# Attention by key heads, with divisions on GpSimd, in one step of a two-layer decoder

## What is computed

```python
def sink_softmax(s, mask, sink):
    s = jnp.where(mask, s, -jnp.inf)
    m = jnp.maximum(jnp.max(s, axis=-1, keepdims=True), sink)
    p = jnp.exp(s - m)
    return p / (jnp.sum(p, axis=-1, keepdims=True) + jnp.exp(sink - m))
# prompt: 4 blocks of 128 queries, each against its own block of keys and the block before
o = einsum(softmax(q k * scale), v);  x = x + o @ w_o
```

## Time and profile before

| | us |
|---|---|
| median of 3 runs | 3200.64 |
| lowest, highest | 3191.85, 3200.99 |
| the profiled execution: its own time | 3202.49 |
| its span, first to last instruction | 3200.7 |
| end of last query tile to first W_O matmul | 1654 to 1801 |

### The profile page before, as it was taken

The page is one execution under the profiler, slowest core; times in us unless marked ns, Lnnn a source line. Parts: engine busy times, 40 slices in busy tenths (PEclk is TensorE's granted clock), DMA queues, the critical chain, the costliest instruction groups (busy, mean ns, idle before and its releaser), DMA issues.

```text
span 3200.7 us, 46734 instructions
## 1 busy us (share of the span) xinstructions
PE 3069.8 (96%) x17222; PEld 2780.8 (87%) x17222; DVE 2551.4 (80%) x4953; ACT 1382.4 (43%) x2559; POOL 1746.1 (55%) x1160
## 2 busy tenths in 40 slices
PE   7879999999999999999888889999999999999997
PEld 7879999999998888888685789999999988888886
DVE  7755999977775999999567358989877759999987
ACT  2522343477764333333344223343777653333332
POOL 4543488887775444443130223788877755544442
PEclk9989999999999999999887899999999999999998
DMA  3212499999999999999130022799999999999993
GB/s 106 77 53 91 128 340 337 339 397 393 393 392 373 401 400 399 401 397 351 53 95 1 27 67 80 274 348 342 371 400 387 395 370 394 399 401 400 398 400 138
DMA packets 286579, 920.92 MB, mean 288 GB/s; under 512 B 27344, under 2 KB 77392, under 8 KB 282688
## 3 DMA queue, kind: packets, MB, share of 16 engines
q1 hardware_dynamic: 154336, 415.63, 35.9%
q0 software_dynamic: 111280, 404.77, 33.4%
q10 hardware_dynamic: 20736, 97.53, 7.4%
HBM read 817.34 MB, written 102.38 MB: 287 GB/s over the span
## 4 chain that ended last, share of the span: by engine, by line
PE 77%; DVE 16%; DMA 3%; POOL 2%; issue 1%; ACT 1%; DVEq 0%; ACTq 0%; SPq 0%
PE ps L1689 34%; PE ps L1637 22%; PE ps L1563 11%; PE ps L1669 5%; POOL low L604 2%; DMA raw<-uT 1%; PE ps L1811 1%; DVE xn L948 1%; DVE xl L941 1%; DVE cand L1218 1%; DVE cand L1225 1%; DVE slot L1231 1%; PE ps L1765 1%; PE ps L1800 1%; DVE rowsB L1129 1%
## 5 line engine op out<-in xcount | busy, mean ns | idle before, releaser
L762 ACT ACTIVATE high<-raw 128x1024 fp32r<-128x1024 f32 x512 | 542.7, 1060 | 992.2 <-PE ps L1689 665.9
L1637 PE MATMUL ps<-xh,high 128*128 128x384 f32 x2048 | 699.1, 341 | 14.8 <-POOL low L604 14.6
L604 POOL TENSOR_TENSOR low<-raw,high 128x1024 fp32r<-128x1024 f32 x256 | 614.2, 2399 | 167.2 <-ACT high L762 160.5
L1637 PE MATMUL ps<-xh,low 128*128 128x384 f32 x2048 | 687.4, 336 | 0.0
L1637 PE MATMUL ps<-xl,high 128*128 128x384 f32 x2048 | 686.2, 335 | 0.0
L1689 PE MATMUL ps<-high,hh 128*128 128x512 f32 x1536 | 483.5, 395 | 7.9 <-DVE low L1301 7.9
L1689 PE MATMUL ps<-low,hh 128*128 128x512 f32 x1536 | 481.1, 394 | 0.0
L1689 PE MATMUL ps<-high,hl 128*128 128x512 f32 x1536 | 480.3, 393 | 0.0
L595 POOL DMA_INDIRECT rowsA<-v,pick x192 | 271.3, 1413 | 296.9 <-DVE ps L1136 288.8
L1637 PEld LDWEIGHTS ps<-xh,high 128*128 128x128 f32 x2048 | 386.1, 189 | 20.8 <-POOL low L604 19.8
L595 POOL DMA_INDIRECT rowsB<-v,pick x192 | 240.2, 1251 | 271.0 <-DVE ps L1136 255.6
(11 more groups left out here) (279 smaller groups left out, 5043.5 us busy)
## 6 DMA issues: line engine op xcount, KB each, us to landing
raw<-uT SPq DMA_DIRECT2D x256, 512.0 KB
raw<-v SPq DMA_DIRECT2D x256, 512.0 KB
gate_dram<-gblk ACTq DMA_DIRECT2D x24, 2048.0 KB
gt<-gate_dram SPq DMA_DIRECT2D x32, 1536.0 KB
s_dram<-sring ACTq DMA_DIRECT2D x120, 384.0 KB
sring<-s_dram SPq DMA_DIRECT2D x120, 384.0 KB
raw<-wts SPq DMA_DIRECT2D x74, 512.0 KB, 3.6
rowsB<-u,pick POOLq DMA_INDIRECT x192
```

Source lines behind the costliest of these rows:

```text
L604: pool.tensor_tensor(low[:, m % 4], raw[:, m % 4], high[:, (m + 2) % 3].bitcast(F32), ALU.subtract).then_inc(sem("lo_ready"), 1)
L762: act.activation(high[:, (m + 2) % 3], tile_raw(m), ACT.Copy).then_inc(sem("hi_ready"), 1)
L1637: ins = pe.matmul(ps[:, m % 2, 0:DN], w[:, c], x[:, c, 0:DN], start=(c == 0 and k == 0), stop=(c == NC - 1 and k == 2))
```

## The change

Units run by key heads: `kv, n = divmod(u, NQB)`, so the units of block 0 are 0, 4, 8 and 12. Their absent half is neither filled, reduced, exponentiated, transposed nor copied. `sbank` swaps its pairs. Scores wait for the rotation of their own key head's two tiles alone. GpSimd multiplies by the reciprocals, and takes the samples' maximum off. `MIX_AT` is 7, two samples a step. `sample_keep` runs in steps 9 and 11. Chunks 0 to 5 are released in step 12 and split in steps 13, 14 and 15 (`SPLIT`), two chunks each. The negated sinks are made once.

```diff
-EXP_AT, SUM_AT_UNIT, TURN_AT, MIX_AT, KEEP_AT = 3, 4, 5, 8, 12
+EXP_AT, SUM_AT_UNIT, TURN_AT, MIX_AT, KEEP_AT, SPLIT = 3, 4, 5, 7, (9, 11), (13, 14, 15)
...
-            return ps[:, 4 * (u % 2):4 * (u % 2) + 2, :]
+            return ps[:, 4 * ((u + 1) % 2):4 * ((u + 1) % 2) + 2, :]
...
+            def weigh(k):
+                p, m = pr[:, k % PRS], sm[:, k % PRS]
+                lo = 0 if k % NQB else WIN
+                pool.wait_ge(sem("p_sum"), k + 1)
+                pool.tensor_tensor(p[:, :, lo:], p[:, :, lo:],
+                                   m[:, 5, 0:GRP].unsqueeze(2).broadcast_to([P, GRP, 2 * WIN - lo]), ALU.mult
+                                   ).then_inc(sem("p_ready"), 1)
+            def weigh_samples(k):
+                if k == EXP_AT:
+                    pool.wait_ge(sem("smax_ready"), 1)
+                    pool.tensor_tensor(pss[:, :, :], pss[:, :, :],
+                                       smS[:, 0].unsqueeze(2).broadcast_to([P, NB, WIN + TS]), ALU.subtract
+                                       ).then_inc(sem("smax"), 1)
+                elif k == SUM_AT_UNIT:
+                    pool.wait_ge(sem("s_sum"), 1)
+                    pool.tensor_tensor(pss[:, :, :], pss[:, :, :],
+                                       smS[:, 5].unsqueeze(2).broadcast_to([P, NB, WIN + TS]), ALU.mult
+                                       ).then_inc(sem("s_ready"), 1)
...
+                if l == 1:
+                    split_weights(W_K, W_O + 2)
+                    for k in range(UNITS):
+                        weigh(k)
+                        weigh_samples(k)
+                    lo = W_O + 2
                 split_weights(lo, hi)
...
+                    if u in SPLIT:
+                        c = 2 * SPLIT.index(u)
+                        split_x(X_O, c, c + 2)
+                split_x(X_O, 2 * len(SPLIT), NC)
...
-                    if not n:
-                        chain.did(dve.memset(p[:, :, 0:WIN], BIG))
-                    chain.did(dve.tensor_reduce(m[:, 0, 0:GRP], p, X, ALU.max))
+                    chain.did(dve.tensor_reduce(m[:, 0, 0:GRP], p[:, :, lo:], X, ALU.max))
...
                 for u in range(UNITS):
-                    normalise(u)
+                    inverse(u)
                     for k in items_due(u):
                         item(k)
...
+                    if u in KEEP_AT:
+                        sample_keep(KEEP_AT.index(u))
+                    if u in SPLIT:
+                        c = 2 * SPLIT.index(u)
+                        for i in range(c, c + 2):
+                            low_half(X_O, i)
+                    if u == SPLIT[0] - 1:
+                        whole(2 * len(SPLIT), u)
                 keep(UNITS - 1)
-                sample_keep(1)
+                whole(NC - 2 * len(SPLIT), UNITS)
+                for c in range(2 * len(SPLIT), NC):
                     low_half(X_O, c)
...
-                pe.wait_ge(sem("roped"), 2 + NC)
...
+                    if n == 0:
+                        pe.wait_ge(sem("roped"), 2 + 2 * (kv + 1))
...
-                    if u >= MIX_AT:
-                        sample_mix(u - MIX_AT)
+                    if MIX_AT <= u < MIX_AT + NB // 2:
+                        sample_mix(2 * (u - MIX_AT))
+                        sample_mix(2 * (u - MIX_AT) + 1)
```

More of the change, by code:

```diff
@@ L321, in decoder @@
         smS = st.take("smS", [P, 6, NB])
+        nsink = st.take("nsink", [P, NH + 1])
         st = Span(nc, free_at, SB_HI)
@@ L656, in high_weight, with split_x @@
                 act.activation(high[:, w % 2], raw[:, w % 2], ACT.Copy).then_inc(sem("qh_ready"), 1)
-            def split_x(k):
-                for c in range(NC):
+            def split_x(k, lo=0, hi=NC):
+                for c in range(lo, hi):
                     act.wait_ge(sem("x_whole"), k * NC + c + 1)
@@ L1394, in attention @@
                 ob = xn
+                chain.did(dve.tensor_scalar(nsink[:, 0:NH], prm[:, P_SINK:P_SINK + NH], -1.0, None, ALU.mult))
+                chain.settle()
                 dve.wait_ge(sem("tile_done"), D_O)
                 def scale_max(k, u):
-                    n, kv = divmod(u, NKV)
+                    kv, n = divmod(u, NQB)
                     p, m = pr[:, u % PRS], sm[:, u % PRS]
@@ L1427, in normalise @@
                     chain.settle()
[L1428 to L1431, removed]
+                    dve.reciprocal(m[:, 5, 0:GRP], m[:, 4, 0:GRP]).then_inc(sem("p_sum"), 1)
                 def keep(u):
-                    n, kv = divmod(u, NKV)
+                    kv, n = divmod(u, NQB)
                     dve.wait_ge(sem("p_out"), u + 1)
@@ L1459, in sample_max, with sample_inverse @@
                     chain.settle()
[L1460 to L1466, removed]
+                    dve.tensor_scalar(smS[:, 3], smS[:, 0], -1.0, prm[:, P_SKS:P_SKS + 1], ALU.mult, ALU.add
+                                      ).then_inc(sem("smax_ready"), 1)
+                def sample_inverse():
                     dve.wait_ge(sem("sexp"), 2)
@@ L1471, in sample_normalise @@
                     chain.settle()
[L1472 to L1476, removed]
+                    dve.reciprocal(smS[:, 5], smS[:, 4]).then_inc(sem("s_sum"), 1)
                 def sample_keep(bb):
@@ L1488, in sample_keep, with whole @@
                     ins.then_inc(sem("s_kept"), 1)
+                def whole(n, u):
+                    dve.wait_ge(sem("s_kept"), 2)
+                    dve.wait_ge(sem("o_copied"), u)
+                    chain.settle()
+                    dve.memset(mark[:, :], 0.0).then_inc(sem("x_whole"), n)
                 def item(k):
@@ L1506, in attention @@
                     if u == SUM_AT_UNIT:
-                        sample_normalise()
-                    if u == KEEP_AT:
-                        sample_keep(0)
-                keep(UNITS - 1)
-                sample_keep(1)
[L1512 to L1516, removed]
+                        sample_inverse()
+                    if u in KEEP_AT:
[6 more added lines that the diff above has]
+                        whole(2 * len(SPLIT), u)
+                keep(UNITS - 1)
+                whole(NC - 2 * len(SPLIT), UNITS)
+                for c in range(2 * len(SPLIT), NC):
                     low_half(X_O, c)
@@ L1783, in item @@
                 def item(k):
+                    if k == 1:
+                        pe.wait_ge(sem("d_free"), D_O - 1)
                     if k >= 2:
@@ L1795, in turn @@
                         pe.wait_ge(sem("prT_ready"), u)
+                    else:
+                        pe.wait_ge(sem("d_free"), D_O)
                     if u in (TURN_AT + 1, TURN_AT + 2):
                         pe.wait_ge(sem("pssT_ready"), u - TURN_AT)
-                    for kb in range(2):
+                    for kb in range(0 if u % NQB else 1, 2):
                         for g in range(GRP):
```

25 lines of the change are left out of this document (12 added, 13 removed).

## The result

The changed kernel takes 3209.51 us (median of 20 runs, 3204.72 to 3220.62), beside 3200.81 for the kernel before (20 runs, 3191.85 to 3216.10): a ratio of 1.0033, 95% interval 1.0021 to 1.0045. The means say +11.0 us (3211.5 against 3200.5, each +-1.2), the medians +8.7. I use means in what follows, since runs of one kernel scatter over 8 to 28 us: the 116 runs of the kernel before in this study have a mean of 3200.9 and a standard deviation of 5.4. Four runs far slower than all others (3447 to 11830 us: one of late_split, one of lag_vector, two of pairs_before) are left out of every figure.

What follows compares the result with a forecast made beforehand. TensorE, busy 96% of the span, was taken as the bound, losing time to waits and its lower clock. Parts gave +4 us, the clock +7: +11 on the profiled 3202.5, or 3211 on the median; range 3199 to 3222.

Steps and rivals of the forecast that it cites:

- Head, -5.7/-6.7: Start to unit 2's transposes: earlier scores and a half unit 0 cut TensorE's idle by 5.7 us (upper clock) or 6.7 (lower).
- Units 3 to 5, -0.5/+2.2: Unit 5 waits longer behind the samples' multiply on GpSimd; together -0.5 us at upper clock, +2.2 at lower.
- The GpSimd multiply, 2.39 us: Weighing by reciprocals on GpSimd, taken as 2.39 us per full unit, against 1.23 on VectorE.
- +6.2: Loop, units 6 to 13: longer path through GpSimd's multiply adds 6.2 us idle at upper clock, 0.5 at lower.
- The end, +7.9/+8.8: Last units to W_O: early split delays units 14 and 15 (idle 7.2, 5.2); net +7.9 us upper, +8.8 lower.
- The clock, +7: Pauses and paired sample outputs lower TensorE's clock: 4 us from unit 13 to W_O, 3 in the middle.
- The sum: Parts at equal clock: +5.9 us upper, +1.0 lower; +4 taken between them by the stage's 0.73.
- W_O starting at the lower level: Sign to look for: W_O starts straight behind the last `mix`, at the lower clock level.
- Rival (4): Early split does not stall because ScalarE is early: +4 becomes about -4, 3197 to 3202; chance 0.26 together with Rival (1).
- Rival (1): Only waits count, clock share stays: +1 to +6 us, 3202 to 3207, no measurable change; chance 0.26 together with Rival (4).
- Rivals (2): Faster: the clock rises early through full units 1 to 3; 3190.5 if 32 us of low work ran high; chance 0.09.
- (3): Heavier: weighing at 2.8 us and the clock low through the end, +23 us, 3224; chance 0.10.

Runs made afterwards that it cites:

- late_split: Changed kernel with all eight chunks split after the last unit, as in the kernel before; mean 3207.7 us, ratio 1.0020 to the kernel before.
- lag_vector: Changed kernel with VectorE's low halves one step after ScalarE's copies and the units' multiply back on VectorE; mean 3203.1 us, ratio 1.0017 to the kernel before.
- pairs_before: Kernel before with only the sample outputs paired in units 7 to 10 and kept in steps 9 and 11; mean 3213.3 us, ratio 1.0037.
- vector_weighs: Changed kernel with the units' multiply back on VectorE, the samples' two passes staying on GpSimd; mean 3206.0 us, ratio 1.0019 to the kernel before.
- pairs_late: Changed kernel with the split after the last unit and the sample output pairs in units 12 to 15; mean 3199.8 us, ratio 0.9990 to the kernel before.
- singles: Changed kernel with the split after the last unit and one sample output per unit from unit 8; mean 3194.1 us, ratio 0.9984 to the kernel before.
- lag_split: Changed kernel with the early split kept but each `xl` one step after its `xh`; mean 3209.7 us, ratio 1.0028 to the kernel before.
- order_only: Changed kernel with late split, one sample output per unit from unit 8, and units' multiply back on VectorE; mean 3197.0 us, ratio 0.9985 to the kernel before.
- fill_before: Kernel before with six dense dummy matmuls ahead of each unit's transposes and twelve ahead of W_O; mean 3201.0 us, ratio 1.0005.
- best_fill: singles with sample copies moved earlier, last copies interleaved with an early split, and dummy matmuls in three long waits; mean 3179.9 us, ratio 0.9934 to the kernel before.

## Why the prediction was right in sum and wrong in its parts

**The time** (3211 for 3209.5), the sign and the chain were right; the shares were not.

- **Head, -5.7/-6.7**: right in place, too large in size. From the end of the last query tile to unit 0's transposes it takes 13.4 us instead of 16.4, 3.0 sooner for 2.7 forecast. PE's waits up to unit 2's transposes went from 11.15 us to 6.81, which is -4.3 where -6.7 was laid out for the lower clock of these rows.
- **Units 3 to 5, -0.5/+2.2**: right; 4.73 us ahead of unit 5, between the 4.1 and 5.8, and +1.4 over the three units.
- **The GpSimd multiply, 2.39 us**: mis-sized. It took 1.89 (1.04 for a half unit), 0.45 under the two-input row that I took it from the earlier trace rows; units 6, 7, 12 and 13 wait 0.57, 0.45, 1.82 and nothing, not 2.0 each, and **+6.2** at the upper clock was too much. Of its cost beside pairs, 5.5 us by vector_weighs, 2.3 us are waits. The trace puts the rest in busy time, but the runs' clock is no higher there (0.9710 for 0.9717), so it stays open.
- **The end, +7.9/+8.8**: this step failed in its cause. The waits came (5.66 and 4.67 for 7.2 and 5.2), but I compared them with the 5.6 us of the kernel before and charged the difference to the early split; late_split has 12.0 us in these places without it. Ahead of units 14 and 15 stand 10.33 us: 1.88 that the kernel before has too, 1.42 for GpSimd's multiply, 3.67 for the split, which saves as much elsewhere, and 3.36 for the cover that the sample outputs had given. The sentence "the three sample outputs that stood in the end are only moved" costed an edit at nothing without asking what they covered there: 1.7 us of PE work ahead of units 14 and 15 each, beside VectorE's copy, sum and multiply. The layout left them out of the end, so their price was in the 13.4 us, under the wrong name; that the size came near is luck in this respect. pairs_before shows these waits in the kernel before, with 6.2 us more waits over the stage.
- **The clock, +7**: right in sign; the size is not confirmed. Two causes were named, the long pauses and "pairs of sample outputs in one piece". The second is the bigger by the runs: 6 to 8 of 12 us in pairs_before, some 6 between pairs_late and singles. In the changed kernel's own trace, its longest run, the clock accounts for some 14 us (12.2 of busy time, and 2 to 4 for the transposes that fell away). All its runs together say less: a clock of 0.9717 for 0.9730 is +4.4 +-1.4 us over the whole execution, the gain at W_O included.
- **The sum**: between +5.9 and +1.0 a clock of 0.73 gives +3.3, not the +4 that was taken. With 4.1 us more waits in the trace, 2 to 4 us fewer transposes and 4.4 us of clock, the change adds up to some 5 to 7 of the measured 11, so the agreement of +4 + 7 with it is in part luck.
- **W_O starting at the lower level**: wrong. It began without a wait, and from 1821 on the clock is 1.00, for 0.94 in the same 52 us before. That gives back some 3 us (0.06 / 0.5 of 52 us done at double price, half of it saved). Why it came back just there is open.
- **Rival (4)**, "without those two waits +4 becomes -4": refuted. Without the early split (late_split) 3.8 us go and with the stall for `xh` taken out (lag_split) 1.8, not 8; the waits shrink by what the split adds and no further.
- **Rival (1)**, waits alone: lost; singles and pairs_late have waits of 27.1 and 28.3 us and means 5.7 us apart.
- **Rivals (2) and (3)**: neither came. In the changed kernel's trace the rows from 1667 to 1691 are at the lower level as before, and the weighing took 1.89 us, not 2.8.

By its parts, then, the change is: order by key heads with its half units, its earlier head, its shorter maximum and the samples' passes on GpSimd, about -4 us (order_only); the multiply on GpSimd, nothing to -3 beside single outputs; the pairs, +13.6 (late_split against singles) or +12.4 (pairs_before); the early split, +3.8 as written. The four are steps along one row of kernels (before, order_only, singles, late_split, after), so their sum, -3.9 - 2.9 + 13.6 + 3.8 = +10.6, is the measured difference by construction and proves nothing; what stands on its own is that pairs_before, outside that row, gives the same price for the pairs.

**Still open**: the pairs' cost divides into 5 to 6 us of waits and 6 to 9 of clock by both pairs of kernels, but a missing cover may lower the clock too, and no run separates that. And what makes runs of one kernel differ by 10 us and more: the clock goes with it (correlation -0.73), but what moves the clock from run to run isn't known. Part of the scatter arises ahead of the change: the stage begins anywhere from 1651.2 to 1662.3 us in the 14 profiled executions, behind the same work in all. fill_before's profiled execution, at 3189.3, was 12 under its mean, so single profiles here rank kernels badly.

## What to carry to other kernels

Work that is "only moved" has two prices: what it covered at its old place, and what it does to the stretch where it goes. Before costing a move at nothing, read what waits behind it in the trace and take its length off that cover. Where a stage mixes small matmuls with waits, count granted clock times busy time, not waits alone: a few dense matmuls in the longest waits paid for themselves here, and the same filling in every unit only broke even. And one part of a change put alone into the kernel before says more than one part taken out of the kernel after.

## What the runs showed of the hardware

**VectorE is held while GpSimd passes.** VectorE's small operation L1451, 0.16 us elsewhere, with two inputs in SBUF:

```profile
1697.14 1.54 DVE L1451 SCALAR_TENSOR_TENSOR sm<-sm,nsink 128x4 f32<-128x4 f32 x1
...
1706.71 0.16 DVE L1451 SCALAR_TENSOR_TENSOR sm<-sm,nsink 128x4 f32<-128x4 f32 x1
...
1712.55 1.29 DVE L1451 SCALAR_TENSOR_TENSOR sm<-sm,nsink 128x4 f32<-128x4 f32 x1
```

```profile
1696.66 2.00 POOL L628 TENSOR_TENSOR pss<-pss,smS 128x1088 f32<-128x1088 f32 x1
...
1711.94 1.89 POOL L620 TENSOR_TENSOR pr<-pr,sm 128x1024 f32<-128x1024 f32 x1
```

Both long ones end within 0.03 us of the end of GpSimd's pass (1698.66 and 1713.83), while the scaling from PSUM and the maximum took their usual 1.21 and 1.22 us beside GpSimd. The Trainium skill's "GPSIMD Engine Reference", section Key points, says that the two contend where a VectorE instruction has two SBUF inputs; the trace agrees, and adds that the small one waited out the whole pass. Two instances are all that the trace has, and what they cost the kernel was not tried.

**A GpSimd pass with one broadcast input is cheaper** than with two full ones: 1.89 us for 128x1024 against 2.34 in the earlier trace rows, so the price of the one isn't that of the other.

**The clock falls in the middle of small matmuls, without a pause.** Sample outputs (two matmuls of 32 columns to a row) in the changed kernel, behind 14 us in which PE never stopped:

```profile
1770.10 0.30 PE L1875 MATMUL ps<-pssN,vnew 8*64 8x32 f32 x2
1770.33 0.42 PE L1873 MATMUL ps<-pssT,vc_sb 128*64 128x32 f32 x2
```

0.30 us for a pair turns into 0.42, and the scores that follow take 3.78 instead of 1.99. The Trainium skill's "TensorE: Matmul & The Clock Gate", section HAM oscillation, has the clock fall when TensorE idles between bursts. What filled waits did agrees with it (0.73 to 0.89 in fill_before, 0.78 to 0.92 in best_fill); this fall inside a full stretch doesn't, and there the row decides.
